# VectorE makes a fourth group of four adaLN units in the first MLP, and the residual returns to SBUF two slabs before the norm

## The reference, cut to what matters

```python
def adaln(cond, w, b):                       # w: 2048 x 12288 a layer; two conditions, c_ctx and c
    m = jax.nn.silu(cond) @ w + b
    return six pieces of 2048: shift, scale, gate of the mixer, then of the MLP

hp = modulate(xp, norm_g[l, 2], sh2p, sc2p)              # rmsnorm(x, g) * (1 + scale) + shift
mp = jnp.square(jax.nn.relu(hp @ w1_mlp[l])) @ w2_mlp[l] # 2048 -> 8192 -> 2048
xp = xp + g2p * rmsnorm(mp, norm_g[l, 3])                # the same for the latent tokens xs
```

## Time and profile before

| | us |
|---|---|
| Median of 3 runs (lowest, highest) | 2489.61 (2489.54, 2492.06) |
| The profiled execution, its own time | 2486.77 |
| Its span in the profile | 2485.0 |
| PE busy in the span | 2428.4 (98%) |
| DVE busy in the span | 1722.3 (69%) |
| ACT busy in the span | 1085.0 (44%) |
| POOL busy in the span | 280.0 (11%) |

### The profile page before, as it was taken

How to read it: one execution, slowest core, us unless ns; L and a number is a source line. 1 busy time by engine, 2 the same in 40 slices (tenths; PEclk the granted TensorE clock), 3 DMA queues, 4 the chain that set the end, 5 groups by cost and what they waited for, 6 DMA issues and landing times.

```text
span 2485.0 us, 37199 instructions
## 1 busy us (share of the span) xinstructions
PE 2428.4 (98%) x13682; PEld 1988.0 (80%) x13682; DVE 1722.3 (69%) x2150; ACT 1085.0 (44%) x1492; POOL 280.0 (11%) x500
## 2 busy tenths in 40 slices
PE   6899999999999999999999999999999999999998
PEld 3577888778788888888887877798888888888887
DVE  2247788587767767775568877675888678564665
ACT  3233443464433433433454456585544344343343
POOL 0032221000100010000012144200001001000000
PEclk8999999999999999999999999999999999999999
DMA  9999999979979988987877956659668668666565
GB/s 359 372 286 332 314 325 316 323 237 311 309 253 298 307 275 274 307 286 256 277 253 243 304 175 224 217 192 301 208 222 276 211 220 277 198 201 203 169 211 163
DMA packets 452295, 651.38 MB, mean 262 GB/s; under 512 B 22360, under 2 KB 308888, under 8 KB 450520
## 3 DMA queue, kind: packets, MB, share of 16 engines
q1 hardware_dynamic: 417952, 535.08, 64.9%
q0 software_dynamic: 31872, 113.51, 13.4%
q10 hardware_dynamic: 2360, 1.32, 0.2%
HBM read 634.39 MB, written 15.43 MB: 261 GB/s over the span
## 4 chain that ended last, share of the span: by engine, by line
PE 87%; DMA 6%; DVE 4%; ACT 2%; issue 1%; SPq 0%; DVEq 0%; ACTq 0%
PE PS L1399 23%; PE PS L1480 13%; PE PS L1481 13%; PE PS L1482 13%; PE PS L1402 12%; PE PS L1428 3%; DMA RAW<-in_w_o_na 2%; DMA RAW<-in_w_qkv_na 1%; DMA SCR<-in_w_ada 1%; DVE WLO L2021 1%; DMA ADW<-in_w_ada 1%; PE PS L1410 1%; PE PS L1412 1%; PE PS L1411 1%; PE PS L1618 1%
## 5 line engine op out<-in xcount | busy, mean ns | idle before, releaser
L2021 DVE TENSOR_TENSOR WLO<-RAW,WHI 128x1024 fp32r<-128x1024 f32 x740 | 873.9, 1225 | 263.7 <-ACT WHI L1734 202.5
L1399 PE MATMUL PS<-HM,WHI 128*128 128x512 f32 x2560 | 648.1, 395 | 2.6 <-issue 2.6
L1734 ACT ACTIVATE WHI<-RAW 128x1024 fp32r<-128x1024 f32 x370 | 390.3, 1055 | 426.2 <-DMA RAW<-in_w_mlp 170.9
L1399 PEld LDWEIGHTS PS<-HM,WHI 128*128 128x128 f32 x2560 | 459.6, 189 | 100.3 <-issue 14.9
L1480 PE MATMUL PS<-WHI,HID 128*128 128x512 f32 x1152 | 450.5, 391 | 0.0
L1481 PE MATMUL PS<-WLO,HID 128*128 128x512 f32 x1152 | 448.4, 389 | 0.0
L1482 PE MATMUL PS<-WHI,HID 128*128 128x512 f32 x1152 | 448.2, 389 | 0.0
L1738 ACT ACTIVATE WHI<-RAW 128x1024 fp32r<-128x1024 f32 x370 | 388.8, 1051 | 98.1 <-DMA RAW<-in_w_mlp 66.6
L1402 PEld LDWEIGHTS PS<-HM,WLO 128*128 128x128 f32 x2560 | 348.9, 190 | 25.6
L1402 PE MATMUL PS<-HM,WLO 128*128 128x256 f32 x2560 | 356.5, 282 | 0.0
L2094 DVE SCALAR_TENSOR_TENSOR X<-X,CS 128x1024 f32<-128x1024 f32 x270 | 334.2, 1279 | 1.3
(11 more groups left out here) (261 smaller groups left out, 1987.4 us busy)
## 6 DMA issues: line engine op xcount, KB each, us to landing
RAW<-in_w_mlp SPq DMA_DIRECT2D x512, 512.0 KB, 5.3
ADW<-in_w_ada SPq DMA_DIRECT2D x106, 1024.0 KB, 10.6
X<-in_w_ada POOLq DMA_DIRECT2D x256, 256.0 KB, 4.3
RAW<-in_w_qkv_na SPq DMA_DIRECT2D x68, 512.0 KB, 9.0
RAW<-in_w_qkvg_gla SPq DMA_DIRECT2D x64, 512.0 KB, 5.5
SCR<-in_w_ada SPq DMA_DIRECT2D x16, 1024.0 KB, 11.5
RAW<-in_w_o_na SPq DMA_DIRECT2D x32, 512.0 KB, 6.8
RAW<-in_w_qkvg_gla SPq DMA_DIRECT2D x64, 256.0 KB, 5.4
```

The lines of the kernel that those rows point to most:

```text
L1399: return mm(bank[:, 0:2 * T2], hi[:, k, P * b:P * b + P], act[:, kc, 0:2 * T2], start=first, stop=False)
L1734: actv(WHI[:, 2 * s + u, 0:HALF], RAW[:, u, 0:HALF], ACT.Copy).then_inc(hi_half, 1)
L2021: tt(WLO[:, 2 * s + u, part], RAW[:, u, part], WHI[:, 2 * s + u, part].bitcast(f32), ALU.subtract).then_inc(done, 1)
```

## The change

`QUADS0` goes from 3 to 4 and `PU` from 6 to 5: each group of MLP0 makes five units on TensorE and four on VectorE, and the unit in output slab 1 goes in all four groups. In the last group the quad's tiles stand one slab earlier than in the others: nine in the hidden phase, four in output slab 0, three in output slab 1 (`LAST_TILES`), the last two of slab 0 behind the biases and the gain. TensorE sums it in slab 2 behind unit 0 and VectorE's turned rows (`mod_done`), not in slab 3; ScalarE stores it in slab 2. X returns only after that. So the gain's first two pieces are loaded ahead of X's return and the other two behind it, and ScalarE's squares of X's pieces 0 and 1 move from slabs 1 and 2 to slab 3. GpSimd's tables for the GLA wait for the quad's row to be stored.

```diff
-        PU = NB + 2
+        PU = NB + 1
-        QUADS0, QUADS1 = HID_GROUPS - 1, 2
+        QUADS0, QUADS1 = HID_GROUPS, 2
...
+            if f == 1:
+                parts = ("y0", "y1", "y2", "x0", "x1", "x2", "g0", "g1", "x3", "g2")
-        PLAN_MLP = ((0,), (1,), (), ())
+        PLAN_MLP = ((0,), (), (), ())
+        LAST_TILES = (4, 3, 0, 0)
+        LAST_UP = KC - sum(LAST_TILES)
...
             pool.wait_ge(hid_done, HID_GROUPS * KC + 2)
+            pool.wait_ge(quad_out, QV * (16 * QU) + 16)
             pool.dma_start(CB[:, 0:768], t_gla).then_inc(sem("gla_in"), 16)
...
                 def between(n, x):      # TensorE, mlp_group
-                    if quads is not None and n == YN - 1 and x == 3:
+                    if quads is not None and norm is None and n == YN - 1 and x == 3:
+                        quad_rows(g + quads, 2 * layer + 3)
+                    if quads is not None and norm is not None and n == 2 and x == 0:
+                        pe.wait_ge(mod_done, 3)
                         quad_rows(g + quads, 2 * layer + 3)
...
+            pe.wait_ge(quad_row, QV + 1)
             turn_rest(2, output_base(M_MLP0))
...
+                if n == YN - 2 and f == 1:      # ScalarE, out_slab
+                    quad_store(QV - 1, QUAD_UNITS[QV - 1])
                 if f is not None and n == YN - 1:
-                    more_squares(f, ("x2", "g0", "g1", "x3", "g2"))
+                    more_squares(f, (("x0", "x1") if f == 1 else ()) + ("x2", "g0", "g1", "x3", "g2"))
                     return
...
-                if 0 < n < YN - 1:
+                if 0 < n < YN - 1 and f != 1:
                     more_squares(f, (("x0",), ("x1",))[n - 1])
...
-                for x in range(1, OUT_TILES[n]):      # VectorE, out_slab
+                more = range(1, out_tiles(quad)[n]) if quad is not None else ()
+                behind = 2 if flush is not None and f is not None else YN + 1
+                for x in more[:behind - 1]:
                     quad_out_tile(quad, n, x)
                 if flush is not None:
                     add_biases(flush)
                     gain_post(*NORM_OF[f])
+                for x in more[behind - 1:]:
+                    quad_out_tile(quad, n, x)
...
+                elif complete:      # VectorE, mlp_group: the last group's hidden phase
+                    hidden_body(g, 0, layer, m, quad, (0, 1), 1)
+                    with dve.Fori(1, NB) as i:
+                        hidden_body(g, i, layer, m, quad, (0, 1), 1)
+                    quad_tile(quad, LAST_UP - 1, (LAST_UP - 1) % 2, NB)
...
+            load_gain(1, (0, 1))      # GpSimd
             return_x(QV)
-            load_gain(1)
+            load_gain(1, (2, 3))
```

More of the change, by code:

```diff
@@ L2095, in quad_tile, with out_tiles @@
                 end.then_inc(quad_step, 1)
+            def out_tiles(q):
+                return LAST_TILES if isinstance(q, int) and q == QV - 1 else OUT_TILES
             def quad_out_tile(q, n, x):
                 if q is not None:
[L2100 removed]
+                    k = KC - sum(out_tiles(q)[n:]) + x
                     quad_tile(q, k, QUAD_SLOT[k], QUAD_SLOT[:k].count(QUAD_SLOT[k]))
@@ L2123, in out_slab @@
                 split_lo(m + 1, 1)
-                quad_out_tile(quad, n, 0)
+                if quad is not None and out_tiles(quad)[n]:
+                    quad_out_tile(quad, n, 0)
                 flush = FLUSH_AT.get((f, n))
@@ L2358, in mlp_group, with hidden_body @@
                              complete and layer and n == YN - 1, quad=quad)
-            def hidden_body(g, i, layer, m, quad=None, tiles=()):
+            def hidden_body(g, i, layer, m, quad=None, tiles=(), ahead=0):
                 for s in range(2):
```

33 lines of the change are left out of this document (17 added, 16 removed).

## The result

The changed kernel took 2492.74 us (median of 22 runs, 2489.15 to 2496.89), the kernel before 2488.55 us beside it (22 runs). The ratio is 1.0017, 95% interval 1.0011 to 1.0023: 4.2 us slower, where 1.0 us faster was forecast; the time lies inside the forecast's range of 2483.0 to 2495.0, on the other side of the kernel before.

The account below looks back on a forecast made before the run. TensorE, busy 98% of the span, was taken as the bound. Groups 0 to 2 give -6.24 us, late weights +3.6, the group's end +1.64: -1.0 us, so 2488.6 us on the median of 2489.61; range 2483.0 to 2495.0.

Parts of the forecast that it names:

- The units removed: TensorE in MLP0: four units go at 2.08 us each, 8.32 us, of which 6.24 in groups 0 to 2.
- Tiles in the hidden phase: Last group's hidden phase: nine tiles on VectorE cost 0, leaving no gap on TensorE; upper bound 7.7 us.
- Tile 12: Output slab 1: tile ends at 1240, next low part at 1243.5, wanted at 1242.85; 0 to 1.5 us stall, taken as 0.
- X's issue: GpSimd in the last group: X's 2 MB return is issued after the quad's sum, near 1254.
- The landings beside X: Last group's output: weight loads beside X's return land 9 to 12 us after issue.
- The rule L + 1.64 for the end: Last group's end: later by weight lateness plus 1.64 us, from squares' 2.45 less VectorE's spare 0.81; bounds 0 and 2.45.
- L: Lateness of slab 3's last weights from X's late return: 3.6 us, bounds -1 and 10.
- seven tiles in output slabs 0 and 1: VectorE in the last group's output: tiles delay low parts, priced at 0 us of TensorE stall, 1.5 kept as bound.
- The bytes of the tiles: Last group's output: 2.6 MB of tile loads come, taken as even with the unit's 2.1 MB leaving SP's queue.
- the 1.7 and 1.1 us: Slab 3's stretch: taken off X's 6.4 us for DMA room from 1276 to 1281 and GLA tables falling behind the weights.
- Rival B: Slab 3: X and gain loads go ahead of the weights whole; zero gain from 4.6 us lateness, up to 2496.0; chance 0.17.
- the rule of the Trainium skill: DMA engines alternate queues by whole packets, so X goes nearly first: weights 6.4 us late, sum +1.8; some 0.15 chance.

Follow-up runs that it names:

- b_squares_only: Kernel before with only ScalarE's four squares of X moved from slabs 1 and 2 to slab 3; 2489.42 us (1.0001).
- b_late_return: Kernel before with X's return held until after unit 0 of slab 2, gain loads split around it, squares in slab 3; 2493.26 us (1.0021).
- a_small_return: Changed kernel with X returned as 128 of its 2048 columns, the rest left out; 2488.59 us (0.9999).
- a_tiles_34_small: Changed kernel with tiles 8 to 15 on 32 columns, 128 of X's 2048 columns returned, tile 12 moved to slab 1; 2485.21 us (0.9985).
- a_thin_tiles_small: Changed kernel with tiles 8 to 15 on 32 of 1536 columns and X returned as 128 of 2048 columns; 2487.02 us (0.9996).
- thin tiles: Changed kernel with tiles 8 to 15 on 32 of 1536 columns: 2492.67 us with X whole, 2487.02 us with 128 of X's 2048 columns.
- the gains soon: Changed kernel with gain loads for slabs 0 to 2 right behind the last tile's load: 1.0028 with X whole, 1.0015 with X's small return.
- a_tiles_34: Complete changed kernel with tile 12 moved from slab 0 to slab 1, X and tiles whole; 2494.67 us (1.0021).
- v2: Changed kernel with 13 tiles in the hidden phase, three in slab 0, sum at slab 1's start, X returned behind it; 2493.05 us (1.0018).
- v3: Changed kernel with 12 tiles in the hidden phase, four in slab 0, none in slab 1; 2491.21 us (1.0013).

## Why the prediction was wrong

**The units removed: right.** 188.05 us a group, 6.2 us in groups 0 to 2. **Tiles in the hidden phase: right**, no gap. **Tile 12:** the forecast of no stall for TensorE held (low part ready at 1233.75, wanted at 1236.16). **X's issue: right**, at 1253.97 for 1254. **The landings beside X: wrong**, 13.4 to 17.0 us for 9 to 12. **The rule L + 1.64 for the end: right**, 6.5 + 1.6 for 8.0. It holds in the other traces too: b_squares_only has -1.6 + 1.6 for 0.0, b_late_return and a_small_return 3.9 + 1.6 for 5.4 and 5.5, a_tiles_34_small 0.2 + 1.6 for 1.7. So the squares' 1.64 us was sized rightly and is in the loss. The 1.6 us by which they let slab 3's weights come sooner (b_squares_only) were not in the working, and no run shows whether the kernel after has them.

**The step that failed is L**, the lateness of slab 3's last weights. It was 3.6, made of X's bytes less what the stretch would give back. The trace has 6.5, and the sum then gives 6.5 - 4.6 = +1.9, which is the trace's +1.8 for MLP0. The medians' +4.2 asks for an L of 8.8 (an estimate, 4.2 + 4.6), which no trace shows. With both causes below out of the way, in a_tiles_34_small, L is 0.2 and the runs give -3.7 [-6.0, -1.5], where the forecast's sum without L is -4.6: the rest of the working stands.

First, "seven tiles in output slabs 0 and 1" was priced by TensorE's slack alone. The working itself had the low part of slab 1's unit 2 begin at 1241.2 instead of 1232.29, 8.9 us late (5.8 measured), found that hardly anybody waits, and put it at 0. A low part has a second customer. It releases the weight buffer, and SP's next load hangs on that. The loads of slab 1 went out 5.8 us late, the transfer engines ran idle there (0.75 and 0.81 for 1.02 and 0.96), and from 40 to 70 us they were full (0.98 to 1.06) and had no room to make it up. By a_thin_tiles_small against a_tiles_34_small this is 4.9 us of the stage, with X's bytes out of the way; by the runs it is 2.7 us, at the edge of what they can tell. VectorE's own work on the tiles was not the cost: with tiles of 0.41 us for 2.48 us the low parts were as late. The bytes of the tiles were set too low as well: 2.6 MB, where the trace has 14 loads of 256 KB, 3.7 MB, issued from 1.7 us ahead of the output to 38.5 us into it.

Second, X. Its late return alone makes the last weights of the kernel before 5.5 us later (b_late_return against b_squares_only, 77.6 for 72.0) and the time 5.0 us longer by the runs. In the kernel after, returning X whole costs 2.5 us by the traces and 4.4 by the runs (a_small_return); with thin tiles it is 1.6 and 5.0, with the gains soon 1.8 and 3.3. So the traces have X cost less where the low parts are late already, and the runs, eleven executions or more each, have 3.3 to 5.0 us in all four pairs. Whether the two causes overlap or add is not shown. Nor does any run show the 1.7 and 1.1 us that the forecast took off X's 6.4 for room in the stretch.

Rival B came out in its direction (L over 4.6) and only in part in its mechanism. Without X's bytes L was still 3.9, and no rival had the idle transfer engines of slab 1. The profiled execution of the kernel after is its fastest run, so the 1.8 us between the traces' difference and the medians' are in no trace and stay open. That they are the same stretch gone worse is likely (traces of close variants had +9.4 and +12.1) but not shown.

By the rule of the Trainium skill (page "DMA: Bandwidth & Descriptors", section "Queues, rings and completion order": an engine takes turns between its queues, a whole packet at a time) the prediction put L at 6.4 us. The trace has 6.5, but the agreement is a chance one: taking X's bytes away left an L of 3.9.

## What to carry to other kernels

When work is put ahead of an instruction that releases a buffer, price the release and not only the consumer's slack: ask what load hangs on it, whether the transfer engines then run idle, and whether the stretch behind has room. Here the wait for a load ahead of such an instruction counted, and the work itself did not. Putting the piece behind the release helped in the cut-down kernel; in the complete one the wait turned up again a slab later (a_tiles_34), so look where the next load will be waited for. Where two causes meet in one full stretch, take each away alone and both together, and set the medians beside the traces before sharing out the loss.

## What the runs showed that I had not expected

A 512 KB weight load, 5.2 us by the median over the whole kernel after, took 16.4 us beside X and the gains, and 8.4 us in the same stretch before. The total rate was the same (375 and 374 GB/s), so the delay is not lost bandwidth but whose bytes go first.

After some of TensorE's waits its granted clock fell from 1.00 to 0.50 (2.4 to 1.2 GHz). In the kernel after, products that are 0.23 us apart stood 0.43 apart for 3.4 us from 1281.7, behind the waits of 2.32 and 2.24 us; the kernel before has no such stretch in its MLPs. Around the 8.61 us wait of v2, which ended at 1221.10, the granted clock was 0.76 and 0.72 over 20 us:

```profile
1211.42:1221.42 10.00, 1.40 (x6) 0.92 (x5) 5.43 (x9) 5.03 (x7) 1.06 (x2) 0.76 0.40 125
1221.42:1231.42 10.00, 10.00 (x58) 7.09 (x57) 9.56 (x9) 4.24 (x4) 1.06 (x2) 0.72 0.89 300
```

In b_late_return one wait of 1.83 us was enough (0.50 from 1286.9 to 1290.3, the wait ended at 1286.07), while v3's wait of 3.08 us had no slow stretch behind it (1.00 from 1270 to 1300). So a wait of TensorE can cost up to half of a slow stretch on top of itself, some 1.6 us for one of 3.4, and not every wait does.
